# Latent attention of a three-block kernel: heads taken in pairs, rotary scores on the two halves of the rows, outputs per query tile

## The reference

```python
def causal_block_attention(q_nope, q_rope, k_nope, k_rope, v):
    ...
        s = jnp.einsum('bhqd,bhkd->bhqk', qn_b, k_nope) + jnp.einsum('bhqd,bkd->bhqk', qr_b, k_rope)
    ...
```

## Time and profile before

| | |
|---|---|
| median of 3 runs | 3281.09 us (3281.01 to 3281.23) |
| span of the profiled execution, first to last instruction | 3270.9 us |
| the attention of block 3 | 2406.2 to 2482.9 us in the span |
| PE busy, whole span | 3179.8 us (97%) |

### The profile page before, as it was taken

The page is one execution under the profiler, slowest core; times in us unless marked ns, Lnnn a source line. Parts: engine busy times, 40 slices in busy tenths (PEclk is TensorE's granted clock), DMA queues, the critical chain, the costliest instruction groups (busy, mean ns, idle before and its releaser), DMA issues.

```text
span 3270.9 us, 35828 instructions
## 1 busy us (share of the span) xinstructions
PE 3179.8 (97%) x14634; PEld 1976.4 (60%) x14634; DVE 1372.5 (42%) x2564; ACT 598.2 (18%) x1240; POOL 1.4 (0%) x6
## 2 busy tenths in 40 slices
PE   8999999999999999999999999999999999999998
PEld 5855554334333433458786588888546444688887
DVE  4256530111111111165743364466353894364655
ACT  2143220110010001121442320102332002120001
POOL 0000000000000000000000000000000000000000
PEclk9999999999999999999997999999999999999999
DMA  6122369999999999931000222222111222222221
GB/s 268 60 78 93 114 250 411 428 428 429 429 428 429 429 428 429 428 138 37 26 1 1 93 87 78 86 95 103 55 52 52 77 77 77 77 78 103 78 78 52
DMA packets 43100, 585.39 MB, mean 179 GB/s; under 512 B 4768, under 2 KB 6816, under 8 KB 7648
## 3 DMA queue, kind: packets, MB, share of 16 engines
q1 hardware_dynamic: 42752, 582.45, 43.8%
q0 software_dynamic: 224, 1.18, 0.1%
HBM read 581.51 MB, written 2.10 MB: 178 GB/s over the span
## 4 chain that ended last, share of the span: by engine, by line
PE 87%; DMA 9%; DVE 3%; ACT 1%; issue 1%; SPq 0%; DVEq 0%; ACTq 0%
PE PS L482 20%; PE PS L294 11%; PE PS L1670 11%; PE PS L686 10%; DMA ring<-in_weights 5%; PE PS L1648 4%; DMA A<-in_weights 4%; PE PS L1246 3%; PE PS L374 2%; PE PS L1593 2%; PE PS L348 2%; PE PS L1634 1%; PE PS L1575 1%; PE PS L2198 1%; PE PS L1038 1%; PE PS L1203 1%
## 5 line engine op out<-in xcount | busy, mean ns | idle before, releaser
L482 PE MATMUL PS<-A 128*128 128x256 f32 x1336 | 298.4, 380 | 0.0
L1670 PE MATMUL PS<-ring,A 128*64 128x512 f32 x1248 | 284.8, 599 | 1.5 <-DMA ring<-in_weights 0.6
L482 PEld LDWEIGHTS PS<-A 128*128 128x128 f32 x1336 | 254.1, 190 | 35.1 <-issue 0.8
L294 PE MATMUL PS<-H,ring 128*128 128x512 f32 x544 | 234.4, 593 | 0.7 <-issue 0.7
L1752 DVE TENSOR_TENSOR A<-A,PS 64x512 f32<-64x512 f32 x64 | 44.1, 690 | 434.6 <-ACT A L1699 434.6
L482 PE MATMUL PS<-H,ring 128*128 128x256 f32 x784 | 185.3, 380 | 0.8 <-ACT A L1785 0.8
L1670 PEld LDWEIGHTS PS<-ring,A 128*64 128x64 f32 x1248 | 82.7, 136 | 168.0 <-issue 160.8
L294 PEld LDWEIGHTS PS<-H,ring 128*128 128x128 f32 x544 | 103.5, 190 | 130.0 <-issue 130.0
L1670 PE MATMUL PS<-A 128*64 128x512 f32 x784 | 178.4, 598 | 2.0 <-DMA A<-in_weights 0.8
L686 PE MATMUL PS<-A 128*128 128x256 f32 x800 | 178.7, 379 | 0.0
L1648 PE MATMUL PS<-A 128*64 128x512 f32 x768 | 174.3, 598 | 3.4 <-DMA A<-in_weights 3.1
(11 more groups left out here) (534 smaller groups left out, 4126.9 us busy)
## 6 DMA issues: line engine op xcount, KB each, us to landing
ring<-in_weights SPq DMA_DIRECT2D x176, 2048.0 KB, 14.2
A<-in_weights SPq DMA_DIRECT2D x96, 2048.0 KB, 24.3
X<-in_x SPq DMA_DIRECT2D x1, 2048.0 KB, 12.9
H<-in_weights SPq DMA_DIRECT2D x1, 2048.0 KB, 13.6
A<-in_weights SPq DMA_DIRECT2D x2, 768.0 KB, 23.8
vec<-in_vec SPq DMA_DIRECT2D x1, 1047.0 KB, 11.1
A<-in_ctx SPq DMA_DIRECT2D x1, 1024.0 KB, 19.1
out_y<-X SPq DMA_DIRECT2D x2, 512.0 KB, 2.9
```

The source lines that it names most:

```text
L294: mm = nc.tensor.matmul(bank[:, 0:out_width], weight_tile(name, n), moving(k), start=k == 0, stop=k == k_tiles - 1)
L482: mm = nc.tensor.matmul(pair_bank(name, p, n), w[:, k, :], x[:, k, :], start=k == 0 and not more, stop=k == 3, skip_group_check=more)
L1670: mm = nc.tensor.matmul(PS[CAP * up:CAP * (up + 1), c % 2, :], XS[:, k, CAP * b:CAP * (b + 1)], expert_tile(slot, 8 * (k % 4) + 4 * up), s ...
```

## The change

A step `s` is now a pair of heads `p` and a query tile `qt`, 16 steps in all. PE computes the two plain scores of a pair one after the other and then the two rotary ones, which lie on different halves of the rows. DVE's mask, maximum, scaling and reciprocal, and ACT's copies of transposes and outputs, take both heads in one instruction; exponentials and normalising stay one for a head. Scores run two steps ahead (4 banks, as before). The output of a query tile is computed one step after its transposes, by one matmul of 128 columns for each key tile, accumulated over the key tiles, where it was four wide ones for a head. `PT_`'s second buffer goes.

```diff
-            for qt in range(TT):
-                score(0, qt)
-            for h in range(heads):
-                for qt in range(TT):
-                    u = TT * h + qt
-                    pe.wait_ge(S["att_probs"], u0 + u + 1)
...
-                    if h + 1 < heads:
-                        score(h + 1, qt)
-                pe.wait_ge(S["att_turned"], u0 + TT * h + TT)
...
-                o = PS[rows(h), 6 + h % 2, :]
-                for kt in range(TT):
-                    mm = nc.tensor.matmul(o[:, kt * P:], v_tok(h, kt), PT_[h % 2][:, kt, kt * P:], start=kt == 0, stop=True,
-                                          skip_group_check=kt > 0)
...
+        def pair_scores(pe, s):
+
+            p, qt = s // TT, s % TT
+            n = (qt + 1) * P
+            bank = lambda b: PS[:, 2 * (s % 2) + b, 0:n]
+            for b in range(2):
+                nc.tensor.matmul(bank(b), a(QN + 2 * p + b)[:, qt * P:n], a(KN + 2 * p + b)[:, 0:n], start=True, stop=False)
+            for b in range(2):
+                mm = nc.tensor.matmul(bank(b), A[half64(b), QR + p, qt * P:n], A[half64(b), KROPE, 0:n],
+                                      start=False, stop=True)
+            mm.then_inc(S["att_scores"], 2)
+
+        def pair_turn(pe, s):
+            pe.wait_ge(S["att_probs"], UNITS2 + 2 * s + 2)
+            if s:
+                pe.wait_ge(S["att_turned"], UNITS2 + 2 * s)
...
+        def pair_output(pe, s):
...
+            for b in range(2):
+                for kt in range(qt + 1):
+                    mm = nc.tensor.matmul(PS[:, 6 + b, qt * P:(qt + 1) * P], VTOK3[:, kt, (2 * p + b) * P:(2 * p + b + 1) * P],
+                                          TURNED[:, 2 * (s % 2) + b, kt * P:(kt + 1) * P], start=kt == 0, stop=kt == qt)
...
+        def attention_tensor(pe):
+            pair_scores(pe, 0)
+            pair_scores(pe, 1)
+            for s in range(STEPS3):
+                pair_turn(pe, s)
+                if s + 2 < STEPS3:
+                    pair_scores(pe, s + 2)
+                if s:
+                    pair_output(pe, s - 1)
+            pair_output(pe, STEPS3 - 1)
...
+        def attention_act(act):
+            pair_exp(act, 0)
+            pair_exp(act, 1)
+            for s in range(STEPS3):
+                n, t = (s % TT + 1) * P, 2 * (s % 2)
+                act.wait_ge(S["att_turn"], UNITS2 + 2 * s + 2)
+                nc.scalar.activation(TURNED[:, t:t + 2, 0:n], PS[:, 4:6, 0:n], ACT.Copy).then_inc(S["att_turned"], 2)
+                if s + 2 < STEPS3:
+                    pair_exp(act, s + 2)
+                if s and s % TT == 0:
+                    pair_leave(act, s // TT - 1)
...
+        def pair_max(dve, s):
...
+            link(dve, "dve", nc.vector.tensor_tensor(own, own, ccol("future", 0, P).unsqueeze(1).to_broadcast([P, 2, P]), ALU.add))
+            link(dve, "dve", nc.vector.tensor_reduce(AMX[:, u:u + 2], PS[:, banks, 0:(qt + 1) * P], AX.X, ALU.max))
+            nc.vector.tensor_scalar(ANM[:, u:u + 2], AMX[:, u:u + 2], -(192 ** -0.5), None, ALU.mult).then_inc(S["att_max"], 2)
+
+        def pair_normalise(dve, s):
+            n, u = (s % TT + 1) * P, 2 * s
+            dve.wait_ge(S["att_exp"], UNITS2 + u + 2)
+            link(dve, "dve", nc.vector.reciprocal(AREC[:, u:u + 2], ASUM[:, u:u + 2]))
+            for b in range(2):
...
+        def attention_dve(dve):
+            pair_max(dve, 0)
+            pair_max(dve, 1)
+            for s in range(STEPS3):
+                pair_normalise(dve, s)
+                if s + 2 < STEPS3:
+                    pair_max(dve, s + 2)
```

More of the change, by code:

```diff
@@ L2187, in three_blocks @@
         PROB = A[:, 24:28, :]
-        PT_ = (A[:, 28:32, :], A[:, 32:36, :])
+        TURNED = A[:, 28:32, :]
         AMX, ANM, ASUM, AREC = (small[:, 256 + 32 * j:288 + 32 * j] for j in range(4))
[L2191 to L2199, removed]
-            for qt in range(TT):
-                score(0, qt)
-            for h in range(heads):
-                for qt in range(TT):
-                    u = TT * h + qt
-                    pe.wait_ge(S["att_probs"], u0 + u + 1)
[L2207 to L2211, removed]
-                    if h + 1 < heads:
-                        score(h + 1, qt)
-                pe.wait_ge(S["att_turned"], u0 + TT * h + TT)
-                if h >= 2:
-                    pe.wait_ge(S["att_heads"], h0 + h - 1)
-                o = PS[rows(h), 6 + h % 2, :]
-                for kt in range(TT):
-                    mm = nc.tensor.matmul(o[:, kt * P:], v_tok(h, kt), PT_[h % 2][:, kt, kt * P:], start=kt == 0, stop=True,
-                                          skip_group_check=kt > 0)
-                mm.then_inc(S["att_out"], 1)
@@ new lines, in three_blocks @@
+        STEPS3, UNITS2 = TT * HEADS3 // 2, TT * HEADS2
+        def pair_scores(pe, s):
[8 more added lines that the diff above has]
+            mm.then_inc(S["att_scores"], 2)
@@ new lines, in pair_turn @@
+        def pair_turn(pe, s):
[3 more added lines that the diff above has]
+            for b in range(2):
+                for kt in range(s % TT + 1):
+                    mm = nc.tensor.transpose(PS[:, 4 + b, kt * P:(kt + 1) * P],
+                                             PROB[:, 2 * (s % 2) + b, kt * P:(kt + 1) * P], ident)
+            mm.then_inc(S["att_turn"], 2)
+        def pair_output(pe, s):
+            p, qt = s // TT, s % TT
+            pe.wait_ge(S["att_turned"], UNITS2 + 2 * s + 2)
+            if p and qt == 0:
+                pe.wait_ge(S["att_heads"], HEADS2 + 2 * p)
+            for b in range(2):
+                for kt in range(qt + 1):
+                    mm = nc.tensor.matmul(PS[:, 6 + b, qt * P:(qt + 1) * P], VTOK3[:, kt, (2 * p + b) * P:(2 * p + b + 1) * P],
+                                          TURNED[:, 2 * (s % 2) + b, kt * P:(kt + 1) * P], start=kt == 0, stop=kt == qt)
+            if qt == TT - 1:
+                mm.then_inc(S["att_out"], 2)
@@ new lines, in attention_tensor, with pair_exp @@
+        def attention_tensor(pe):
[8 more added lines that the diff above has]
+            pair_output(pe, STEPS3 - 1)
+        def pair_exp(act, s):
+            n = (s % TT + 1) * P
+            act.wait_ge(S["att_max"], UNITS2 + 2 * s + 2)
+            for b in range(2):
+                u, t = 2 * s + b, 2 * (s % 2) + b
+                nc.scalar.activation(PROB[:, t, 0:n], PS[:, t, 0:n], ACT.Exp, scale=192 ** -0.5, bias=ANM[:, u:u + 1],
+                                     accum_out=ASUM[:, u:u + 1]).then_inc(S["att_exp"], 1)
@@ new lines, in pair_leave @@
+        def pair_leave(act, p):
+            act.wait_ge(S["att_out"], HEADS2 + 2 * p + 2)
+            nc.scalar.activation(A[:, QN + 2 * p:QN + 2 * p + 2, :], PS[:, 6:8, :], ACT.Copy).then_inc(S["att_heads"], 2)
+        def attention_act(act):
[9 more added lines that the diff above has]
+                    pair_leave(act, s // TT - 1)
+            pair_leave(act, HEADS3 // 2 - 1)
@@ new lines, in pair_max @@
+        def pair_max(dve, s):
+            qt, u = s % TT, 2 * s
+            banks = slice(2 * (s % 2), 2 * (s % 2) + 2)
+            dve.wait_ge(S["att_scores"], UNITS2 + u + 2)
+            own = PS[:, banks, qt * P:(qt + 1) * P]
+            link(dve, "dve", nc.vector.tensor_tensor(own, own, ccol("future", 0, P).unsqueeze(1).to_broadcast([P, 2, P]), ALU.add))
+            link(dve, "dve", nc.vector.tensor_reduce(AMX[:, u:u + 2], PS[:, banks, 0:(qt + 1) * P], AX.X, ALU.max))
+            nc.vector.tensor_scalar(ANM[:, u:u + 2], AMX[:, u:u + 2], -(192 ** -0.5), None, ALU.mult).then_inc(S["att_max"], 2)
@@ new lines, in pair_normalise @@
+        def pair_normalise(dve, s):
+            n, u = (s % TT + 1) * P, 2 * s
+            dve.wait_ge(S["att_exp"], UNITS2 + u + 2)
+            link(dve, "dve", nc.vector.reciprocal(AREC[:, u:u + 2], ASUM[:, u:u + 2]))
+            for b in range(2):
+                prob = PROB[:, 2 * (s % 2) + b, 0:n]
+                nc.vector.tensor_scalar(prob, prob, AREC[:, u + b:u + b + 1], None, ALU.mult).then_inc(S["att_probs"], 1)
+        def attention_dve(dve):
[5 more added lines that the diff above has]
+                    pair_max(dve, s + 2)
@@ L2254, in att_normalise @@
                                     ).then_inc(S["att_probs"], 1)
[L2256 to L2273, removed]
         half64 = lambda h: slice(64 * (h % 2), 64 * (h % 2) + 64)
@@ L2288, in three_blocks @@
         MIX2 = [RT, RT + 1, RT + 2, MQ, MQ + 1, MQ + 2, MU, MU + 1]
-        UNITS2 = TT * HEADS2
         def moba_score(pe, u):
@@ L2932, in three_blocks @@
         ROUND = 1.5 * 2.0 ** 23
-        full = lambda h: slice(0, P)
-        mla_parts = lambda h: [(a(QN + h), a(KN + h)),
-                               (A[half64(h), QR + h // 2, :], A[half64(h), KROPE, :])]
         def third_tensor(pe):
@@ L2972, in third_tensor @@
             pe.wait_ge(S["roped"], 5)
```

(6 more changed lines are left out.)

## The result

The changed kernel takes 3287.14 us (median of 21 runs) where the kernel before takes 3281.01 (21 runs): a ratio of 1.0021, 95% interval 1.0015 to 1.0028. It is slower, by about 6 us. The forecast, 3295.3 us, had the right sign and more than twice the loss that came (14.2 us for 6.1).

The account below looks back on a forecast made before the run. PE's work bounded the kernel; after the change, PE's waits for DVE in the attention would. From the median, 3281.09 + 6.3 (waits) + 7.9 (clock falls) = 3295.3 us, range 3284.5 to 3306.

Parts of the forecast that it names:

- The closed loop: Attention of block 3: PE's transposes wait each step for DVE's normalising, queued behind a later maximum; 19.8 us a pair, before 18.0.
- The loop's +6.3 us: Attention of block 3, end to end: the next product starts at 2489.2 against 2482.91, 6.3 us later.
- tail: End of the attention: from the last exponentials' and normalising's end, transposes, outputs and copy take 7.0 us.
- the 0.3 taken for hand-overs: Each attention step: late score result 0.18 us, two semaphores and an exposed weight load about 0.12 (estimate).
- Row halves overlap: Rotary scores of both heads run at once on PE's row halves, saving 2.1 us a pair at full overlap.
- Changes of row count: PE's scores: one change for a step, not one for a unit, saving 1.2 us a pair.
- Outputs cost the same columns and are hidden: Attention outputs on PE: 20 records a head cost 2.2 us, no change, and lie beside DVE's part.
- The clock's +7.9 us: Attention stage: waits bring two clock falls of 12 us, a third of that time lost; bounds nothing and +14.5.
- loop as above, clock stays: Attention stage: same waits for DVE but clock stays at 2.4 GHz; 3287.4 us, likely 3285 to 3290; chance 0.20.

Follow-up runs that it names:

- outputs twice: Every output matmul issued twice, against the changed kernel: 3296.6 us, a ratio of 1.0057 to the kernel before.
- the second one: The changed kernel, unchanged, run again for a second profile: 3291.24 us.
- b_again: The kernel before, unchanged, run again for a second profile: 3279.77 us, with a span of 3278.0.
- the third of before: The kernel before, unchanged, run for a third profile: its attention stage takes 79.3 us; no whole time is given.

## Why the prediction was wrong in its size

- **The closed loop: right.** The waits stand where they were put, ended by DVE's normalising, and the normalising ahead of the maximum takes them away by order alone. A pair takes 20.16 us against 19.8 forecast; the longest wait in it is 2.28 against 2.5, all its waits 4.6 against 5.6.
- **The loop's +6.3 us: a little low.** In the first profile after, a pair with a fall (2456.99 to 2478.89) takes 21.90, so a fall of 3.4 us costs 1.7; the first pair's step with a fall costs 1.7 as well. Without both the stage is 84.8 us, 8.1 above rows 3 and 4. The missing 1.8 are 0.1 in each step and a tail of 7.4 us for 7.0. In the 0.3 taken for hand-overs, 0.12 stood on no row; in the step with 512 keys DVE's mask starts 0.12 us behind the last score's columns and the transposes 0.05 behind the normalising.
- **Row halves overlap: right, and fully.** Changes of row count were halved at about the price taken: the scores of 512 keys of a pair take 2.87 us (2442.42 to 2445.29), 2.84 by the forecast's terms.
- **Outputs cost the same columns and are hidden: right** (outputs twice).
- **The clock's +7.9 us on top of the median: this step failed.** It took two falls of 12 us in the new stage at a third of their length each; the first profile after has two of 3.4, at half their length 3.4 us of time in all, and the second one 6.5 (91.3 less 84.8). And it counted falls on one side only. The stage before was taken as free of them, from a profile that happened to be; in the two other profiles of before a fall behind the tail's waits costs 2.6 us. The rows came from an execution of 3272.7 us, but the sum started at the median, 3281.09, on the ground that 10.2 us lay outside the instructions; 1.8 do. The median already held falls, and the forecast added the new ones to it without taking off the old. Over the whole execution little is left of the term: the mean granted clock (of which 0.001 is worth some 3 us, an estimate) is 0.987 in the profile behind the forecast, 0.985 and 0.984 in the other two of before, 0.985 and 0.983 in the two after; of 21 runs after 15 have 0.985, and of the 21 of before beside `b_again` 18 have 0.984.
- **What the tally is.** Between the second profile of before and the first one after: attention 0.5 us later, stage 79.3 to 88.2 (+8.9), and a fall at 2870 that only the former has (-1.7): 7.7 us of span (3278.0 to 3285.7). Between the third of before and the second after it is 11.7. The medians differ by 6.1; the changed kernel's runs spread over several us (3285.08 to 3290.88), and the difference between its loop's 8.1 and the 6.1 was not placed.
- **The rival "loop as above, clock stays"** gave 3287.4. The time agrees, its reason does not: the clock did fall, and the loop cost more; what it left out on both sides happened to cancel, so that it came this close is luck.

## What to carry to other kernels

A lead in one engine's program is worth only what the other engines' orders leave of it: with in-order engines, follow one unit round all of them and look for an instruction that waits for work of a later unit and has work of an earlier one queued behind it. Here swapping two calls on VectorE turned a loss of 6 us into a gain of 7. Before a sum is made against a median, ask whether the profiled execution is a usual one (its time beside the runs; here time less span is 1.7 to 1.9 us in every run that gives both), and charge a clock that falls to both sides.

## What the runs showed of the hardware that was not expected

- Two 64-row float32 matmuls on the two halves of the rows run fully side by side, though the program writes one head's matmul ahead of the other's: 1.13 us for four records of 512 columns, 1.12 for two.
- Behind the same wait, at the same place, the granted clock fell in one execution and not in another (the tail of the kernel before: not in the first profile, 6.9 and 6.8 us at 0.50 in the others). Falls account for at least 4.3 of the 7.1 us between the first two profiles of before: 2.6 there and 1.7 at 2870.
- With the rotary scores apart the stage spent 47.7 of 114.8 us at 1.2 GHz, with them paired 6.8 of 88.2 in the first profile.
